# Attention stage: the weighted sum of values right behind each block of scores on TensorE

## The chip, the cores and the metric

The kernel runs on one core of one Trainium2 chip. The metric is the device time of one launch in microseconds, as the median of several runs. The before kernel was run three times.

## What is computed

One layer of a hybrid block on x of 2048 positions by 1024, all in float32. The part that matters here is the attention over a sliding window of two chunks of 64 positions, with 8 query heads and 2 key/value heads:

```python
def window_sink_attention(q, k, v, sinks):
    ...
    qc = q.reshape(B, n_chunks, CHUNK, KV_HEADS, GQA_GROUP, HEAD_DIM)
    kw = chunk_window(k.reshape(B, n_chunks, CHUNK, KV_HEADS, HEAD_DIM))
    vw = chunk_window(v.reshape(B, n_chunks, CHUNK, KV_HEADS, HEAD_DIM))
    scores = jnp.einsum('bnqkgd,bnjkd->bnkgqj', qc, kw).astype(jnp.float32) * scale
    ...
    probs = jax.nn.softmax(jnp.concatenate([scores, sink], axis=-1), axis=-1)[..., :-1]
    out = jnp.einsum('bnkgqj,bnjkd->bnqkgd', probs.astype(v.dtype), vw)
```

Around it stand: z = RMSNorm(x) @ w_in, split into q, k, v and the two halves u and v of a gating unit; rotary embedding of q and k; the gating unit; both parts normalised, concatenated and multiplied by w_out; a residual; and a SwiGLU block of width 2816 with another residual.

## The kernel before, in words

Each engine has its program written out by hand, and semaphores join them. Nothing reorders anything: an instruction starts when those ahead of it on its engine have been issued and its own waits hold. Float32 matrix products are split into a high and a low part, so each product is three matmuls (high x high, high x low, low x high). Pairs of tiles go through a Strassen-like scheme of seven products instead of eight.

The 2048 positions are 16 tiles of 128. The stages on TensorE are: the gating unit's columns of w_in, then the attention stage, in which the product with the q, k, v columns of w_in for pair p = j + 1 is laced with the attention of tiles 2j and 2j + 1, then the product with w_out, then the SwiGLU block's up and down products. The loop of the attention stage (from line 2243) runs over j = 0 to 6, some 22 us each.

The steps for tile k, and the engine of each:

- `rope_products` (VectorE, L1510 and L1517) multiply z by the rope table into `ropeA` and `ropeB`; `rotate` (GpSimd) adds these into `qrot` (L651) and `krot` (L654).
- `turn_qk` (TensorE, L2155 and L2157) transposes `qrot` into PSUM tile `T0` and `krot` into `T1`. It waits for `rot_done`, and for `aO_done`, since `T0` also holds the result of `weighted`.
- `queries` (ScalarE, L933) and `keys` (VectorE, L1526 to L1528) copy these to SBUF.
- `scores` (TensorE, L2172) makes the scores in PSUM tile `S`: 64x64 blocks of the array with 128 columns moving. It waits until both halves of `probsT` of tile k - 1 have been copied.
- `maxima` (VectorE, L1536 to L1543) and `exps` (ScalarE, L942 to L944) make `probs`.
- `turn_probs` (TensorE, L2181) transposes `probs`; one half is copied into `probsT` by ScalarE (L952), the other by VectorE (L1549).
- `weighted` (TensorE, L2196) multiplies `probsT` by the values `vA` and `vB` into `T0`: 128x64 blocks with 64 columns moving, 16 instructions. It waits for `probsT`, for the values, and for `queries` of the tile whose transposes were in `T0`.
- `attended` (VectorE, L1560) divides by the sums of exponentials into `aO` and frees `T0`; then come `squares_A` (ScalarE, L958, L960), `rms_A` (GpSimd, L603) and `mix_A` (VectorE, L1569).

The seven products (`qkv_product(p, i)`, L2141 to L2143) have 12 matmuls each of 128x128 with 384 columns. `qkv_u2` and `qkv_u3` (VectorE, L1476, L1483) read products 2 and 3; `qkv_upper` (VectorE, L1491) reads product 5 and completes z of the next even tile, and `rope_products` of that tile comes right behind it, then `qkv_lower` (L1495), which reads product 6, then `attended(2j)`. Behind `attended(2j)` VectorE has in most iterations one or two operations of another kind: `again_scale` (L1607, at the start of iterations 1 and 3), `wout_lo_part` (L1573, at the start of iterations 2 and 4, and more in 7), `again_sums` (L1615, L1617, iteration 5), `left_lo` (L1261, iteration 6). The prediction names the six moved even blocks by their j, 0 to 5; the operation behind `attended(2j)` then stands at the start of iteration j + 1.

Of the kernel before, what the change touches and what calls it, by code (L numbers as in the profile page):

```python
# [15 lines left out]
TILES = SEQ // P  # L16
# [19 lines left out]
NP = TILES // 2  # L36
# [11 lines left out]
def build_kernel(nc, x, x_q, w_uv, w_qkv, w_out, w_gu, w_dn, gain_in, gain_out, post_mix, pre_ffn,  # L48
# [206 lines left out]
    def chunk(c):  # L255
        return slice(c * P, (c + 1) * P)
# [22 lines left out]
    with block:  # L279
# [1727 lines left out]
        def _(e):  # L2007
# [107 lines left out]
            def qkv_product(p, i, ks=range(HK)):  # L2115
                b, (left, _) = (p + 1) % 2, UP_PRODUCTS[i]
                if ks[0] == 0:
                    if p == 0:
                        e.wait_ge(w_split, 9 + i + 1)
                        if i in (0, 1):  # L2120
                            e.wait_ge(sB_done, 2 * (NP - 1))
                        if i == 2:
                            e.wait_ge(gel_done, 4 * (NP - 1) + 2)
                        if i == 3:
                            e.wait_ge(v12_first, NQ)
                    else:
                        if i == 0 and p < NP - 1:
                            e.wait_ge(hl_in[b], 32 * ((p + 1) // 2))
                        if p == NP - 1 and i in (0, 1, 3):
                            e.wait_ge(lsplit, 3 * NP + (1, 2, 0, 3)[i])  # L2130
                        if i < 4:
                            e.wait_ge((z11_done, v12_first, u2_first, v21_first)[i], (0, NQ, NQ, NQ)[i] + p)
                    if i in (4, 5):
                        e.wait_ge(in_copied, 2 * (NQ + p) + i - 3)
                    if i == 6:
                        e.wait_ge(u3_first, NQ + p + 1)
                bank = QB[BANK[i]]
                for k in ks:
                    w = slice(k * P, (k + 1) * P)
                    hi, lo = lb_hi[b][:, left, w], lb_lo[b][:, left + 1, w]  # L2140
                    e.matmul(bank, hi, wq_hi[i][:, k, :], start=i < 4 and k == 0, stop=False, skip_group_check=True)  # L2141
                    e.matmul(bank, hi, wq_lo[i][:, k, :], start=False, stop=False, skip_group_check=True)
                    ins = e.matmul(bank, lo, wq_hi[i][:, k, :], start=False, stop=k == HK - 1, skip_group_check=True)  # L2143
                if ks[-1] == HK - 1:
                    ins.then_inc(in_done, 1)

            def turn_qk(k):
                e.wait_ge(rot_done, 2 * k + 2)
                if k:
                    e.wait_ge(aO_done, k - 1)  # L2150
                    e.wait_ge(k_done, 3 * k)
                if k == TILES - 2:
                    e.wait_ge(mixT_split, 2)
                for i in range(PAIRS):
                    ins = e.transpose(T0[:, chunk(i)], qrot[:, chunk(i)], ident[:, :])  # L2155
                ins.then_inc(q_full, 1)
                e.transpose(T1[:, 0:P], krot[:, :], ident[:, :]).then_inc(k_full, 1)  # L2157

            def scores(k):
                if k == 0:  # L2160
                    e.wait_ge(pool_consts, 6)
                    e.wait_ge(sB_done, TILES)
                else:
                    e.wait_ge(pTa_done, k)
                    e.wait_ge(pTv_done, k)
                e.wait_ge(qT_done, k + 1)
                e.wait_ge(k_done, 3 * k + 2)
                for i in range(PAIRS):
                    for half, window in enumerate((kA[k % 2], kB)):
                        for kv in range(KVH):  # L2170
                            r = slice(kv * HD, (kv + 1) * HD)
                            ins = e.matmul(S[half * CH:(half + 1) * CH, kv, chunk(i)],  # L2172
                                           qT[r, i * P + half * CH:i * P + (half + 1) * CH], window[r, :],
                                           start=True, stop=True)
                ins.then_inc(s_full, 1)

            def turn_probs(k):
                for i in range(2):
                    e.wait_ge(exp_done, 9 * k + 5 + 4 * i)
                    for c in range(4):  # L2180
                        ins = e.transpose(S[:, i, chunk(c)], probs[:, chunk(4 * i + c)], ident[:, :])  # L2181
                    ins.then_inc(pT_full, 1)

            def weighted(k):
                e.wait_ge(pTa_done, k + 1)
                e.wait_ge(pTv_done, k + 1)
                e.wait_ge(v_done, 3 * k + 3)
                e.wait_ge(qT_done, min(k + 2, TILES))
                if k == TILES - 4:
                    e.wait_ge(mixT_split, 1)  # L2190
                if k == TILES - 2:
                    e.wait_ge(mixT_split, 3)
                for h in range(NH):
                    kv = h // PAIRS
                    for half, vals in enumerate((vA[k % 3], vB[k % 2])):
                        ins = e.matmul(T0[half * CH:(half + 1) * CH, h * HD:(h + 1) * HD],  # L2196
                                       probsT[:, h * P + half * CH:h * P + (half + 1) * CH],
                                       vals[:, kv * HD:(kv + 1) * HD], start=True, stop=True)
                ins.then_inc(pv_done, 1)

            def mix_transposes(k):
                e.wait_ge(mix_in[k % 2], 16 * (k // 2 + 1))
                if k < 2:
                    e.wait_ge(qT_done, TILES - 2 + 2 * k)
                    e.wait_ge(k_done, 3 * (TILES - 2 + 2 * k))
                if k:
                    e.wait_ge(mixT_split, 2 * k)
                if k == 2:
                    e.wait_ge(aO_done, TILES)
                for i in range(2):  # L2210
                    for c in range(4):
                        ins = e.transpose(T[i][:, chunk(c)], mixin[k % 2][:, chunk(4 * i + c)], ident[:, :])
                    ins.then_inc(mixT_full, 1)

            def out_units(k, first, end):
                par = k % 2
                if first == 0:
                    e.wait_ge(mixT_split, 2 * k + 2)
                    if k == 0:
                        e.wait_ge(z11_done, NP)  # L2220
                        e.wait_ge(v12_first, NQ + NP)
                    if k == 1:
                        e.wait_ge(u2_first, NQ + NP)
                        e.wait_ge(v21_first, NQ + NP)
                    if k >= 2:
                        e.wait_ge(y_done, k - 1)
                for unit in range(first, end):
                    c, a = unit // 2, unit % 2
                    w = slice(a * 512, (a + 1) * 512)
                    if k == 0 and a == 0:  # L2230
                        e.wait_ge(wout_split, c + 1)
                    ins = three(M[par][:, a, :], mixT_hi[par][:, chunk(c)], mixT_lo[par][:, chunk(c)],
                                wout_hi[c][:, w], wout_lo[c][:, w], c == 0, c == KD - 1)
                    if k == TILES - 1 and c in (3, 4) and a == 1:
                        ins.then_inc(wout_half, 1)
                if end == 2 * KD:
                    ins.then_inc(mm2_full, 1)
# [5 lines left out]
            for j in range(NP - 1):  # L2243
                p = j + 1
                qkv_product(p, 0)
                turn_qk(2 * j)
                if j:
                    turn_probs(2 * j - 1)
                qkv_product(p, 1, range(0, 2))
                scores(2 * j)  # L2250
                qkv_product(p, 1, range(2, 4))
                qkv_product(p, 2)
                if j:
                    weighted(2 * j - 1)
                qkv_product(p, 3)
                turn_qk(2 * j + 1)
                qkv_product(p, 4, range(0, 2))
                turn_probs(2 * j)
                qkv_product(p, 4, range(2, 4))
                scores(2 * j + 1)  # L2260
                if p == NP - 1:
                    mix_transposes(0)
                qkv_product(p, 5)
                qkv_product(p, 6)
                weighted(2 * j)
            out_units(0, 0, 2)
            turn_probs(TILES - 3)
            out_units(0, 2, 5)
# [151 lines left out]
```

## Time and profile before

| what | value |
|---|---|
| runs | 1850.42, 1850.9, 1851.03 us |
| median | 1850.9 us |
| profiled execution, first to last instruction (its span) | 1849.8 us |
| TensorE busy | 1824.4 us, 99% of the span |
| VectorE busy | 1273.8 us, 69% |
| ScalarE busy | 743.1 us, 40% |
| GpSimd busy | 154.0 us, 8% |
| attention stage | about 203 to 402 us |

The profile is of one execution on the one core. A time of its own outside the span is not listed for it, so the span stands for it. Busy means that at least one instruction is in the engine; for TensorE the granted clock is at full speed in all 40 slices. A matmul's listed duration is its latency; the pace at which matmuls follow each other is read from their starts. Behind most rows of a timeline nothing stands; "[0.24 <-PE T L2196]" says that the engine was idle for 0.24 us ahead of it and that the matmuls of line 2196 on tile T ended that.

### The profile page before, as it was taken

What the parts mean: (1) busy time and instruction counts of PE and PEld (TensorE: products, weight loads), DVE (VectorE), ACT (ScalarE), POOL (GpSimd) and SP (SyncE); (2) the same over time, 40 slices, a digit from 0 to 9 for tenths busy, and PEclk for the clock granted to TensorE, in tenths of its full rate; (3) what the DMA queues carried; (4) which work ended last, traced back from release to release, by engine and by line L of the source; (5) the groups of instructions that cost most, each with busy time, mean ns of one, the idle gap of its engine ahead of it and who ended that gap; (6) DMA issues with size and microseconds to landing.
All of it is one profiled execution on the core that took longest, in us unless ns stands there. A gap on an engine that the chain in (4) does not pass through costs nothing.

```text
span 1849.8 us, 24806 instructions
## 1 busy us (share of the span) xinstructions
PE 1824.4 (99%) x9322; PEld 1526.0 (82%) x9322; DVE 1273.8 (69%) x1625; ACT 743.1 (40%) x1279; POOL 154.0 (8%) x162
## 2 busy tenths in 40 slices
PE   9999899999999999999999999999999999999998
PEld 7788899978888888888888888888887888888887
DVE  7878877864458867676777767777677756554574
ACT  7776566753345332323224332322323222232342
POOL 1211222211000000000000000000000000000244
PEclk9999999999999999999999999999999999999999
DMA  6787645245576323332235423333234754535655
GB/s 229 291 291 276 238 186 198 92 160 193 200 274 246 139 85 108 122 101 95 85 110 196 148 85 99 114 105 108 85 108 166 268 219 163 189 132 179 244 203 190
DMA packets 134324, 310.78 MB, mean 168 GB/s; under 512 B 6384, under 2 KB 85232, under 8 KB 121072
## 3 DMA queue, kind: packets, MB, share of 16 engines
q1 hardware_dynamic: 134256, 309.90, 47.8%
q8 instruction: 40, 0.66, 0.1%
q14 instruction: 28, 0.23, 0.0%
HBM read 207.64 MB, written 102.24 MB: 168 GB/s over the span
## 4 chain that ended last, share of the span: by engine, by line
PE 75%; DVE 2%; issue 0%; POOL 0%; ACT 0%; DVEq 0%; POOLq 0%
PE T L2010 7%; PE T L2012 7%; PE T L2011 7%; PE ZB L2332 4%; PE ZB L2334 4%; PE ZB L2333 4%; PE T L2334 4%; PE T L2332 4%; PE T L2333 4%; PE S L2334 3%; PE S L2332 3%; PE S L2333 3%; PE ZA L2334 3%; PE ZA L2332 3%; PE ZA L2333 3%; PE ZA L2012 1%
## 5 line engine op out<-in xcount | busy, mean ns | idle before, releaser
L2010 PE MATMUL T<-tb_hi,sb_hi 128*128 128x512 f32 x616 | 239.9, 390 | 1.5 <-DVE sb_lo L1896 1.2
L2012 PE MATMUL T<-tb_hi,sb_lo 128*128 128x512 f32 x616 | 239.7, 389 | 0.0
L2011 PE MATMUL T<-tb_lo,sb_hi 128*128 128x512 f32 x616 | 239.6, 389 | 0.0
L1184 ACT ACTIVATE sb_hi<-sb_raw 128x1408 fp32r<-128x1408 f32 x56 | 77.4, 1382 | 291.0 <-PE T L2012 275.6
L1759 DVE TENSOR_TENSOR t_lo<-t_raw,t_hi 128x1024 fp32r<-128x1024 f32 (+1 forms) x126 | 168.9, 1396 | 0.1
L2010 PEld LDWEIGHTS T<-tb_hi,sb_hi 128*128 128x128 f32 x616 | 115.6, 188 | 26.6 <-issue 2.1
L2332 PE MATMUL ZB<-s_hi,t_hi 128*128 128x512 f32 x352 | 137.1, 389 | 0.3 <-DVE t_lo L1759 0.3
L2332 PE MATMUL T<-s_hi,t_hi 128*128 128x512 f32 x352 | 137.0, 389 | 0.0
L2334 PE MATMUL T<-s_hi,t_lo 128*128 128x512 f32 x352 | 136.9, 389 | 0.0
L2334 PE MATMUL ZB<-s_hi,t_lo 128*128 128x512 f32 x352 | 136.9, 389 | 0.0
L2333 PE MATMUL ZB<-s_lo,t_hi 128*128 128x512 f32 x352 | 136.9, 389 | 0.0
L2333 PE MATMUL T<-s_lo,t_hi 128*128 128x512 f32 x352 | 136.9, 389 | 0.0
L2011 PEld LDWEIGHTS T<-tb_lo,sb_hi 128*128 128x128 f32 x616 | 115.7, 188 | 24.0
L2012 PEld LDWEIGHTS T<-tb_hi,sb_lo 128*128 128x128 f32 x616 | 115.6, 188 | 23.9
L1896 DVE TENSOR_TENSOR sb_lo<-sb_raw,sb_hi 128x1408 fp32r<-128x1408 f32 x56 | 96.2, 1717 | 34.5 <-ACT sb_hi L1184 34.5
L1124 ACT ACTIVATE th<-v 128x512 f32<-128x512 f32 x66 | 41.8, 633 | 192.2 <-DVE v L1785 90.1
L702 POOL TENSOR_TENSOR rstdf<-msf,mhalf 128x1 f32<-128x1 f32 x16 | 14.5, 904 | 1182.2 <-ACT msf L1193 1180.0
L1111 ACT ACTIVATE p<-T 128x512 f32<-128x512 f32 x22 | 13.2, 598 | 245.5 <-PE T L2334 245.5
L2332 PE MATMUL ZA<-s_hi,t_hi 128*128 128x512 f32 x264 | 102.7, 389 | 0.0
L2333 PE MATMUL ZA<-s_lo,t_hi 128*128 128x512 f32 x264 | 102.7, 389 | 0.0
L2332 PE MATMUL S<-s_hi,t_hi 128*128 128x512 f32 x264 | 102.7, 389 | 0.0
L2333 PE MATMUL S<-s_lo,t_hi 128*128 128x512 f32 x264 | 102.7, 389 | 0.0
(311 smaller groups left out, 4283.6 us busy)
## 6 DMA issues: line engine op xcount, KB each, us to landing
t_raw<-w_gu SPq DMA_DIRECT2D x42, 1024.0 KB, 4.7
act_d<-ac SPq DMA_DIRECT2D x22, 1792.0 KB, 8.0
sb_raw<-act_d SPq DMA_DIRECT2D x56, 704.0 KB, 4.1
h_d<-quarters SPq DMA_DIRECT2D x8, 1792.0 KB, 6.6
s_raw<-h_d SPq DMA_DIRECT2D x14, 1024.0 KB, 6.3
lb_hi<-hl_d SPq DMA_DIRECT2D x6, 1792.0 KB, 7.2
lb_lo<-hl_d SPq DMA_DIRECT2D x6, 1792.0 KB, 10.7
tb_raw<-w_dn SPq DMA_DIRECT2D x6, 1536.0 KB, 6.5
```

The source lines that it names most:

```text
L702: e.tensor_tensor(rstdf[:, f % 2:f % 2 + 1], msf[:, f % 2:f % 2 + 1], mhalf[:, 0:1], ALU.pow).then_inc(rstdf_ready, 1)
L1111: e.activation(p1[:, :], GU[u][0], ACT.Copy).then_inc(pcopy_done, 1)
L1124: e.activation(th[i][:, :], src, ACT.Tanh, scale=0.5).then_inc(th_done, 1)
L1184: e.activation(sb_hi[it % 2][:, :, :], sb_raw[it % 2][:, :, :], ACT.Copy).then_inc(sb_hi_done, 1)
L1759: e.tensor_tensor(t_lo[u][:, first:end, :], t_raw[u][:, first:end, :], t_hi[u][:, first - 1:end - 1, :].bitcast(F32), ALU.subtract).then_i ...
L1896: e.tensor_tensor(sb_lo[it % 2][:, :, :], sb_raw[it % 2][:, :, :], sb_hi[it % 2][:, :, :].bitcast(F32), ALU.subtract).then_inc(sb_split, 1)
L2010: e.matmul(out_ap, lhi, rhi, start=start, stop=False)
L2011: e.matmul(out_ap, lhi, rlo, start=False, stop=False)
L2012: return e.matmul(out_ap, llo, rhi, start=False, stop=stop)
L2332: e.matmul(bank, hi, s_hi[i][:, :, w], start=i < 4 and k == 0, stop=False, skip_group_check=True)
L2333: e.matmul(bank, hi, s_lo[i][:, :, w], start=False, stop=False, skip_group_check=True)
L2334: ins = e.matmul(bank, lo, s_hi[i][:, :, w], start=False, stop=k == HK - 1, skip_group_check=True)
```

## The change

On TensorE alone, in the attention stage's loop, `weighted` goes to another place. `weighted(2j - 1)` stood behind product 2 of the next pair and now stands right behind `scores(2j)`. `weighted(2j)` stood behind product 6, at the end of the iteration, and now stands right behind `scores(2j + 1)`, ahead of products 5 and 6. The last iteration (p = 7) keeps `weighted(12)` behind product 6; there `mix_transposes(0)` stays behind `scores(13)`. So six blocks of odd tiles (1, 3, 5, 7, 9, 11) and six of even tiles (0, 2, 4, 6, 8, 10) move. No instruction is added or taken away, and waits stay as they were.

```diff
                 qkv_product(p, 1, range(0, 2))
                 scores(2 * j)
+                if j:
+                    weighted(2 * j - 1)
                 qkv_product(p, 1, range(2, 4))
                 qkv_product(p, 2)
-                if j:
-                    weighted(2 * j - 1)
                 qkv_product(p, 3)
                 turn_qk(2 * j + 1)
                 qkv_product(p, 4, range(0, 2))
                 turn_probs(2 * j)
                 qkv_product(p, 4, range(2, 4))
                 scores(2 * j + 1)
-                if p == NP - 1:
+                if p < NP - 1:
+                    weighted(2 * j)
+                else:
                     mix_transposes(0)
                 qkv_product(p, 5)
                 qkv_product(p, 6)
-                weighted(2 * j)
+            weighted(TILES - 4)
```

TensorE before, from `scores(3)` to `turn_qk(4)` (S and T0 are the PSUM tiles, wq_hi5, wq_hi6 and wq_hi0 the weights of products 5, 6 and 0; of each run of like rows the first and last stand):

```order
L2172 MATMUL S<-kB_150,qT_147 64x128 x2
L2141 MATMUL ZA<-wq_hi5_122,lb_hi1_75 128x384
...
L2141 MATMUL ZB<-wq_hi6_123,lb_hi1_75 128x384
...
L2196 MATMUL T0<-vA2_153,probsT_157 64x64
...
L2141 MATMUL ZA<-wq_hi0_117,lb_hi0_74 128x384
...
L2155 MATMUL T0<-ident_253,qrot_146 128x128 x4
```

The `weighted` block stands between product 6 and product 0. Now:

```order
L2172 MATMUL S<-kB_150,qT_147 64x128 x2
L2196 MATMUL T0<-vA2_153,probsT_157 64x64
...
L2141 MATMUL ZA<-wq_hi5_122,lb_hi1_75 128x384
...
L2141 MATMUL ZB<-wq_hi6_123,lb_hi1_75 128x384
...
L2141 MATMUL ZA<-wq_hi0_117,lb_hi0_74 128x384
...
L2155 MATMUL T0<-ident_253,qrot_146 128x128 x4
```

The block has moved ahead of product 5, and between product 5 and the turn only products 6 and 0 are left. For the odd tiles, TensorE before, from `scores(2)` to product 3:

```order
L2172 MATMUL S<-kB_150,qT_147 64x128 x2
L2141 MATMUL ZA<-wq_hi1_118,lb_hi1_75 128x384
...
L2141 MATMUL ZB<-wq_hi2_119,lb_hi1_75 128x384
...
L2196 MATMUL T0<-vA1_152,probsT_157 64x64
...
L2141 MATMUL ZB<-wq_hi3_120,lb_hi1_75 128x384
```

And now:

```order
L2172 MATMUL S<-kB_150,qT_147 64x128 x2
L2196 MATMUL T0<-vA1_152,probsT_157 64x64
...
L2141 MATMUL ZA<-wq_hi1_118,lb_hi1_75 128x384
...
L2141 MATMUL ZB<-wq_hi2_119,lb_hi1_75 128x384
...
L2141 MATMUL ZB<-wq_hi3_120,lb_hi1_75 128x384
```

Here the block has moved ahead of the second half of product 1 and of product 2. The order of the other engines' instructions is the same as before.

## Rows read from the trace of the kernel before

**Rows 1.** The page, busy us, share of the span, instructions of each engine.
```profile
PE 1824.4 (99%) x9322; PEld 1526.0 (82%) x9322; DVE 1273.8 (69%) x1625; ACT 743.1 (40%) x1279; POOL 154.0 (8%) x162
```

**Rows 2.** Line 2155 (`turn_qk`): what ended its engine's idle time, us, times.
```profile
  POOL krot L654: 3.1, 5
```

**Rows 3.** Timeline, `weighted(3)`: start us, duration us, engine, line, operation, out<-in.
```profile
239.56 0.33 PE L2142 MATMUL ZB<-wq_lo,lb_hi 128*128 128x384 f32 x1
239.73 0.34 PE L2143 MATMUL ZB<-wq_hi,lb_lo 128*128 128x384 f32 x1
240.00 0.27 PE L2196 MATMUL T<-vA,probsT 128*64 128x64 f32 x1
...
240.93 0.22 PE L2196 MATMUL T<-vB,probsT 128*64 128x64 f32 x1
...
241.08 0.44 PE L2141 MATMUL ZB<-wq_hi,lb_hi 128*128 128x384 f32 x1
241.36 0.34 PE L2142 MATMUL ZB<-wq_lo,lb_hi 128*128 128x384 f32 x1
```

**Rows 4.** Timeline of TensorE, the end of `scores(5)` and the next product.
```profile
270.50 0.28 PE L2172 MATMUL S<-kB,qT 64*64 64x128 f32 x2
270.71 0.44 PE L2141 MATMUL ZA<-wq_hi,lb_hi 128*128 128x384 f32 x1
```

**Rows 5.** Timeline of TensorE at the stage's end, `scores(15)` and `weighted(14)`.
```profile
389.12 0.28 PE L2172 MATMUL S<-kB,qT 64*64 64x128 f32 x2
389.32 0.27 PE L2196 MATMUL T<-vA,probsT 128*64 128x64 f32 x1
```

**Rows 6.** Timeline at j = 5, VectorE's copy of `probsT` and the start of `scores(11)`.
```profile
336.95 0.68 DVE L1549 COPY probsT<-S 128x512 f32<-128x512 f32 x1
...
337.76 0.33 PE L2172 MATMUL S<-kA,qT 64*64 64x128 f32 x2
```

**Rows 7.** Timeline at j = 2, from product 5 to `turn_qk(6)`.
```profile
273.10 0.56 DVE L1491 TENSOR_TENSOR z<-ZA,au 128x384 f32<-128x384 f32 x1 [0.47 <-PE ZA L2143]
...
275.65 1.28 POOL L651 TENSOR_TENSOR qrot<-ropeA,ropeB 128x512 f32<-128x512 f32 x1 [4.91 <-DVE ropeB L1517]
...
276.28 0.69 DVE L1560 TENSOR_TENSOR aO<-T,rden 128x512 f32<-128x512 f32 x1 [0.24 <-PE T L2196]
...
276.88 1.22 DVE L1607 TENSOR_TENSOR xa_raw<-xa_raw,gq 128x1024 f32<-128x1024 f32 x1
276.89 1.53 POOL L654 TENSOR_TENSOR krot<-ropeA,ropeB 128x128 f32<-128x128 f32 x1
...
278.18 0.34 PE L2143 MATMUL ZA<-wq_hi,lb_lo 128*128 128x384 f32 x1
...
278.47 0.33 PE L2155 MATMUL T<-ident,qrot 128*128 128x128 f32 x1
```

**Rows 8.** Timeline at j = 1, from product 5 to `turn_qk(4)`.
```profile
250.47 0.56 DVE L1491 TENSOR_TENSOR z<-ZA,au 128x384 f32<-128x384 f32 x1 [0.49 <-PE ZA L2143]
...
254.26 1.55 DVE L1573 SCALAR_TENSOR_TENSOR wout_lo<-wout_raw,gcol_out,wout_hi 128x1024 fp32r<-128x1024 f32 x1
254.27 0.46 POOL L654 TENSOR_TENSOR krot<-ropeA,ropeB 128x128 f32<-128x128 f32 x1
...
255.72 0.60 PE L2155 MATMUL T<-ident,qrot 128*128 128x128 f32 x4
```

**Rows 9.** Timeline at j = 6, GpSimd's rotation and VectorE's `wout_lo`.
```profile
368.35 1.29 POOL L651 TENSOR_TENSOR qrot<-ropeA,ropeB 128x512 f32<-128x512 f32 x1 [6.69 <-DVE ropeB L1517]
368.65 2.07 DVE L1573 SCALAR_TENSOR_TENSOR wout_lo<-wout_raw,gcol_out,wout_hi 128x1024 fp32r<-128x1024 f32 x1
369.59 1.45 POOL L654 TENSOR_TENSOR krot<-ropeA,ropeB 128x128 f32<-128x128 f32 x1
```

**Rows 10.** Timeline at j = 4, the same two engines.
```profile
322.34 0.68 DVE L1615 TENSOR_TENSOR lb_raw<-xa_raw,xa_raw 128x512 f32<-128x512 f32 x1
322.34 1.00 POOL L654 TENSOR_TENSOR krot<-ropeA,ropeB 128x128 f32<-128x128 f32 x1
```

## Prediction

> **What bounds the kernel now.** I read the page's busy shares first: TensorE is busy for 1824.4 of 1849.8 us, so its own sequence of instructions, plus the few places where it waits, is the time [rows 1]. The page's row of granted clock is at full speed in every slice, so no term here hangs on the clock. The edit reaches only the loop of the attention stage, about 205 to 370 us, where tile k's `turn_qk`, `turn_probs`, `scores` and `weighted` are laced between the seven products of the next pair. Second I read who made the transposes of `turn_qk` wait: five times GpSimd's `krot`, 3.1 us in all with the weight loads' waits [rows 2]; three of them are turns of this loop. The profile thus names GpSimd's rotation as the wait that already ends last at some turns. Third come the timelines at one joint of each kind, to price what is moved; last, those of VectorE and GpSimd in front of a waiting turn.
>
> **What a `weighted` block costs where it stands now.** The last product matmul starts at 239.73, the block's first at 240.00, its last at 240.93; the next product starts at 241.08, its second matmul at 241.36 [rows 3]. That is 0.27 + 0.93 + 0.15 + 0.28 = 1.63 us. Without the block the same two steps are two product pitches of 0.17 (239.56 to 239.73), 0.35 us. The block costs 1.28 us: 0.93 of its own and 0.35 of entering and leaving. All twelve moved blocks read alike.
>
> **What it costs behind `scores`.** From the last `scores` to a product is 0.21 us, with the slow second step behind it too [rows 4]. At the end of the stage the kernel already has a `scores` with a `weighted` right behind, and there that step is 0.20 us [rows 5]. In its new place a block adds 0.20 + 0.93 + 0.15 - 0.21 = 1.07 us; the slow second step is paid once, where it was paid twice. A joint therefore saves 1.28 - 1.07 = 0.21 us of TensorE's own time, and twelve save 2.5 us. That much the change gives by itself.
>
> The Trainium skill, "TensorEngine Tiling (Array Packing)", Key Properties, says that changing the tiling mode drains TensorE. Products, `scores` (64x64) and `weighted` (128x64) are three shapes, so by this rule the joint keeps three of four drains; the trace agrees in kind, since 0.20 us stays between the two small blocks.
>
> **The odd tiles: the saving stays.** `weighted(2j-1)`, six blocks, moves inside the stretch from `scores(2j)` to `scores(2j+1)`. Its data are there, because `scores(2j)` waits for the same halves of `probsT`. Its reader on VectorE, `attended`, has `qkv_u2` ahead of it, which waits for product 2 and now comes 1.07 us later; `attended` ends some 1.5 us behind product 2's last matmul, and the next `turn_qk`, which waits for it, is 2.4 us behind. So 0.8 us of cover is left. `scores(2j+1)` waits a little for `probsT`, but that chain starts at `turn_qk(2j+1)`, which moves with TensorE. One exception, at j = 5: VectorE has extra sums behind `attended`, so `qkv_u3` loses the start 0.21 us earlier, and from there VectorE runs without a gap up to the copy of `probsT` that starts at 336.95; `scores(11)` starts at 337.76, right behind it [rows 6]. I take 0.2 us off. Sum: 6 x -0.21 + 0.2 = -1.05 us.
>
> **The even tiles: the cover of GpSimd's rotation goes.** `weighted(2j)`, six blocks (j = 0 to 5), stood behind product 6, between product 5 and `turn_qk(2j+2)`. It now stands ahead of product 5. But product 5 starts a chain that ends in that turn: VectorE adds `z` (L1491, 273.10), multiplies by the rope table, GpSimd adds `qrot` from 275.65 to 276.93 and `krot` from 276.89 to 278.42, and `turn_qk` starts at 278.47 [rows 7]. I count from the start U of L1491. The chain lets the turn start at U + 5.37 here, while TensorE would have been ready 0.12 us sooner, at U + 5.25 (a turn that does not wait follows the product by 0.17, this one by 0.29). The change takes 1.28 us out of TensorE's side of this race and nothing out of the chain's: TensorE is ready at U + 3.97, and the turn still comes when `krot` is done. The 1.07 us ahead of product 5 moves U itself later and is paid in full.
>
> What does the chain take then? `krot` lasts 1.53 us here and not its median 0.46, since VectorE's operation with two SBUF inputs started 0.01 us ahead of it, and it ended 0.32 us behind that operation's end at 278.10 [rows 7]. At j = 1 (and 3) the order is the other way: `wout_lo` and `krot` start within 0.01 us, `krot` lasts 0.46 and ends at U + 4.26, a whole 1 us before the turn at U + 5.25 [rows 8]. After the change this cannot stay: `attended` waited 0.24 us for the `weighted` block [rows 7] and now need not, so the VectorE operation behind it starts at least that much sooner, while `qrot` still runs. The one place of that kind is j = 6: `wout_lo` came 0.30 us after `qrot`'s start, took 2.07 us, and `krot` ended at 371.04, which is 1.40 us behind `qrot`'s end at 369.64 [rows 9]. With that row as price, `krot` ends at U + 3.83 + 1.40 and the turn starts at U + 5.28, for j = 0, 1, 2, 3 and 5. For j = 4 the VectorE operation takes 0.68 and not 1.27 us [rows 10], so U + 4.69.
>
> Against the distances of now this is -0.09 for j = 0, 2, 5 (5.37 before), +0.03 for j = 1, 3 and -0.56 for j = 4 (5.25 before). A turn that waited is also 0.05 us longer than one that did not (the block of five transposes reads 0.49 against 0.44 between first and last start), new for j = 1, 3, 4: +0.15. Sum of the even tiles: 6 x 1.07 - 0.27 + 0.06 - 0.56 + 0.15 = +5.8 us. TensorE then waits some 1.3 us at five turns and 0.7 at one. Nothing behind takes this back: what follows a turn (`keys`, `queries`, copies of `probsT`) hangs on it, the loads of the next pair are issued a whole pair ahead, and the later stages are TensorE's.
>
> Bounds. If `krot` kept its place ahead of `wout_lo` at j = 1 and 3, each of these turns would start at U + 4.31, 2 x 0.97 = 1.9 us less. If it went first everywhere, the even tiles would cost 6 x 1.07 + 3 x (4.31 - 5.37) + 3 x (4.31 - 5.25) + 0.15 = +0.6. If VectorE's operation had to wait out `qrot` and then took its whole 1.22 to 1.27 us, where row 9 shows 1.08 left of it, 0.15 to 0.2 us is added at five turns, +0.9. I take row 9, the only one in which VectorE's operation comes while `qrot` runs.
>
> The Trainium skill, "SBUF — State Buffer", Who interferes with whom, states that a VectorE instruction with two SBUF inputs and a GpSimd one that reads SBUF block each other for the whole instruction, by order of issue. By this rule it would be the upper bound of the paragraph above; row 9's 2.07 us is less than a whole wait (0.99) and a whole operation (1.27), so the row stands.
>
> **Total.** +5.8 - 1.05 = +4.8 us on the profiled span of 1849.8, so a span near 1854.6. The median of three runs, 1850.9, lies 1.1 us over the span, which I carry over: 1855.7 us, 0.26% slower. A measurement of this kernel can tell about 0.2%, 3.7 us, from no change.
>
> **Rivals.**
> - *`krot` stays first at j = 1 and 3.* It ended 1 us before its turn now, and 0.01 us decides who goes first. For it: [rows 8] itself. Against: VectorE's operation starts at least 0.24 us sooner. Time: 4.8 - 1.9 = +2.9 us, 1853.8.
> - *No joint waits, only the saving shows (not slower).* It decides at 1.3 us: the chain from product 5 to `krot` would have to end by U + 3.97. For it: TensorE's own time does fall by 12 x 0.21. Against: even with no VectorE operation in its way the chain ends at U + 4.26. Time: -2.5 us, 1848.4; with the freed `krot` everywhere +0.6 - 1.05, about 1850.5.
> - *The joints save nothing and the block is total.* The 0.20 us of [rows 5] is one place, ahead of other products. If the new joints cost what two entries cost, the odd tiles give 0 instead of -1.05, the even ones 1.28 instead of 1.07, and +0.9 comes from the full block: 4.8 + 1.05 + 1.3 + 0.9 = +8.0, 1858.9.
> - *The change does not do what it says.* The order shows TensorE's rows moved as told and no other engine's, so only its worth is open.
>
> **How the numbers follow.** The forecast (1855.7, from +3.8 to +6.2) gets 0.6, `krot` first 0.2, the two forms without a cost together 0.11, the dear joint 0.06, something that gains more than 3.7 us 0.03. The range runs from 1852.7 to 1857.8: it holds the forecast and the first rival with the full block's bound, about 0.84. Slower by over 0.2% needs more than 3.7 us: 0.6 + 0.06, 0.66. Within 0.2%: 0.31. Faster: 0.03.
>
> **What would show it.** Right: `turn_qk` waits for `krot` at six even turns, 0.7 to 1.4 us each, where three waited 0.12; `krot` lasts over 1 us at j = 1 and 3; `scores` to `weighted` reads 0.20 and the second step behind the pair 0.28; the stretch from `turn_qk(2j)` to `turn_qk(2j+2)` is longer by 0.3 to 1.0 us. Wrong: `krot` at 0.46 with a small wait (first rival), or a turn 0.17 us behind product 0 (second). A new wait of a product, of `scores` or of VectorE's `keys` on something else would mean that I missed a chain.

## The result and the profile after

The changed kernel takes 1856.35 us (median of 7 runs, 1855.85 to 1857.37) against 1851.03 us (7 runs) of the kernel before: ratio 1.0028, 95% interval 1.0019 to 1.0037, so about 5.3 us slower. The profiled span is 1854.6 us against 1849.8, +4.8.

The page of the changed kernel, busy us of each engine, beside [rows 1]:

```profile
PE 1823.9 (98%) x9322; PEld 1527.5 (82%) x9322; DVE 1274.0 (69%) x1625; ACT 743.7 (40%) x1279; POOL 154.9 (8%) x162
```

TensorE is busy for 0.5 us less and the span is 4.8 us longer: what was added is waiting. The waits of TensorE between 225 and 365 us in the changed kernel (engine, tile, line, whom it waited for: us in all, times, longest), where the kernel before lists none:

```profile
PE T L2155 <- POOL krot L654: 6.5, 6, 1.2
PE S L2172 <- ACT probsT L952: 0.2, 1, 0.2
```

Six turns of even tiles wait for GpSimd's `krot`. The timeline of the changed kernel at j = 1, to be laid beside [rows 8] (start us, duration us, engine, line, operation, in brackets the idle time before it and its releaser):

```profile
252.96 0.56 DVE L1491 TENSOR_TENSOR z<-ZA,au 128x384 f32<-128x384 f32 x1 [1.57 <-PE ZA L2143]
...
255.51 1.29 POOL L651 TENSOR_TENSOR qrot<-ropeA,ropeB 128x512 f32<-128x512 f32 x1 [6.01 <-DVE ropeB L1517]
...
255.81 0.68 DVE L1560 TENSOR_TENSOR aO<-T,rden 128x512 f32<-128x512 f32 x1
256.41 1.47 DVE L1573 SCALAR_TENSOR_TENSOR wout_lo<-wout_raw,gcol_out,wout_hi 128x1024 fp32r<-128x1024 f32 x1
...
256.75 0.34 PE L2143 MATMUL ZA<-wq_hi,lb_lo 128*128 128x384 f32 x1
256.76 1.44 POOL L654 TENSOR_TENSOR krot<-ropeA,ropeB 128x128 f32<-128x128 f32 x1
...
258.25 0.66 PE L2155 MATMUL T<-ident,qrot 128*128 128x128 f32 x4 [1.16 <-POOL krot L654]
```

`attended` (L1560) no longer has an idle time ahead of it, so `wout_lo` starts at 256.41, while `qrot` runs until 256.80 (255.51 + 1.29). `krot`, which lasted 0.46 us in [rows 8], now lasts 1.44, and the turn starts 5.29 us behind L1491; it was 5.25. TensorE's last product matmul had started at 256.75, 1.50 us before the turn, where 0.17 is no wait. At j = 4 the operation in front is the short one, beside [rows 10]:

```profile
327.29 0.93 DVE L1615 TENSOR_TENSOR lb_raw<-xa_raw,xa_raw 128x512 f32<-128x512 f32 x1
...
327.63 0.91 POOL L654 TENSOR_TENSOR krot<-ropeA,ropeB 128x128 f32<-128x128 f32 x1
```

And the new joint, `scores(3)` with `weighted(2)`, beside [rows 4, 5]:

```profile
249.26 0.28 PE L2172 MATMUL S<-kB,qT 64*64 64x128 f32 x2
249.47 0.27 PE L2196 MATMUL T<-vA,probsT 128*64 128x64 f32 x1
...
250.40 0.22 PE L2196 MATMUL T<-vB,probsT 128*64 128x64 f32 x1
250.55 0.45 PE L2141 MATMUL ZA<-wq_hi,lb_hi 128*128 128x384 f32 x1
250.83 0.34 PE L2142 MATMUL ZA<-wq_lo,lb_hi 128*128 128x384 f32 x1
```

0.21 + 0.93 + 0.15 us, and the slow second step of 0.28 once: the joint is as cheap as foreseen.

### The profile page after: what moved, and what is told of

Read it like the earlier page. It is cut to its first block, busy times and chain, and to the rows that moved or that the text cites. A ratio compares the mean times of both kernels' runs of the same rounds, so it can differ in the third digit from the quotient of the medians.

```text
span 1854.6 us, 24806 instructions
## 1 busy us (share of the span) xinstructions
PE 1823.9 (98%) x9322; PEld 1527.5 (82%) x9322; DVE 1274.0 (69%) x1625; ACT 743.7 (40%) x1279; POOL 154.9 (8%) x162
## 4 chain that ended last, share of the span: by engine, by line
PE 76%; DVE 3%; ACT 1%; issue 0%; POOL 0%; DVEq 0%; POOLq 0%; ACTq 0%
PE T L2010 7%; PE T L2012 7%; PE T L2011 7%; PE ZB L2334 4%; PE ZB L2336 4%; PE ZB L2335 4%; PE T L2336 4%; PE T L2334 4%; PE T L2335 4%; PE S L2336 3%; PE S L2334 3%; PE S L2335 3%; PE ZA L2336 3%; PE ZA L2334 3%; PE ZA L2335 3%; PE ZB L2010 2%
## 5 line engine op out<-in xcount | busy, mean ns | idle before, releaser
L2336 PE MATMUL ZA<-s_hi,t_lo 128*128 128x512 f32 x264 | 102.7, 389 | 0.0
```

What stands on the lines that cost most here:

```text
L2336: ins = e.matmul(bank, lo, s_hi[i][:, :, w], start=False, stop=k == HK - 1, skip_group_check=True)
```

## The experiments

Nine kernels ran, eleven times each (e2 six times), beside runs of the kernel before on the same chip. A median here can tell about 1.7 us from no change (2.4 in e2), so small differences are also read from the profile, as the time from the start of `turn_qk(0)` to the start of `turn_probs(15)`, the attention stage without what lies around it. That stretch is 182.83 us before (212.49 to 395.32) and 187.81 in the changed kernel (213.08 to 400.89).

| kernel | median, us | against before | ratio, 95% interval | stretch, us | against before |
|---|---|---|---|---|---|
| the change | 1856.35 | +5.3 | 1.0019 to 1.0037 | 187.81 | +4.98 |
| e1_odd_only | 1849.69 | -1.1 | 0.9987 to 1.0005 | 181.80 | -1.03 |
| e2_even_only | 1856.75 | +5.95 | 1.0020 to 1.0045 | 188.82 | +5.99 |
| e3_after_krot_first | 1850.37 | -0.4 | 0.9990 to 1.0008 | 182.39 | -0.44 |
| e4_after_ops_later | 1851.95 | +1.15 | 0.9997 to 1.0015 | 183.81 | +0.98 |
| e5_even_behind_product5 | 1850.17 | -0.3 | 0.9989 to 1.0007 | 182.23 | -0.60 |
| e6_odd_krot_first | 1849.10 | -1.4 | 0.9983 to 1.0001 | 181.34 | -1.49 |
| e7_after_probs_first | 1849.15 | -1.35 | 0.9983 to 1.0001 | 181.17 | -1.66 |
| e8_all_parts | 1848.31 | -2.2 | 0.9979 to 0.9997 | 180.60 | -2.23 |
| e9_krot_first | 1849.88 | -0.7 | 0.9988 to 1.0006 | 182.07 | -0.76 |

(Before, on the three chips: 1850.8 for e1 to e4, 1850.5 for e5 to e7, 1850.54 for e8 and e9.)

**The two halves of the change, each alone: e1 and e2.**

The edit of e1, to the kernel before:

```diff
                 scores(2 * j)
+                if j:
+                    weighted(2 * j - 1)
                 qkv_product(p, 1, range(2, 4))
                 qkv_product(p, 2)
-                if j:
-                    weighted(2 * j - 1)
```

And that of e2, to the kernel before:

```diff
                 scores(2 * j + 1)
-                if p == NP - 1:
+                if p < NP - 1:
+                    weighted(2 * j)
+                else:
                     mix_transposes(0)
                 qkv_product(p, 5)
                 qkv_product(p, 6)
-                weighted(2 * j)
+            weighted(TILES - 4)
```

> The kernel before with only the six odd blocks, weighted(2j-1), moved behind scores(2j). Theory (the joint saves TensorE 0.21 us each, and the loss is all on the even side): about -1.0 us against before, the stretch from scores(2j) to scores(2j+1) shorter by 0.2 us, and the waits on krot as before (three of 0.12 us). Rival (a block behind scores costs more than it saves, in both places): +2 us or more.

> The kernel before with only the six even blocks, weighted(2j), moved behind scores(2j+1), ahead of product 5. Theory (the block goes to the other side of product 5, whose chain through VectorE and GpSimd sets the even turn): +5.8 us against before, all in waits of turn_qk(2j+2) on krot, 1.2 us at five turns and 0.6 at one. Rival (the joint itself is dear): the stretch lengthens in TensorE's own steps, and odd and even blocks each bring half of the loss.

Measured: -1.1 and +5.95 us; in the stretch -1.03 and +5.99, together +4.96, for +4.98 of the whole change. In e1 the way from `scores(2j)` to `scores(2j+1)` is 11.19 us (235.88 to 247.07) from `scores(2)` and 11.21 to 11.29 from the others, where it was 11.38 or 11.39. In e2 the waits between 225 and 365 us are these alone:

```profile
PE T L2155 <- POOL krot L654: 6.4, 6, 1.2
```

The loss is all on the even side, and there it is the turn's wait.

**Is it the end of GpSimd's rotation? e3 and e4.** e3 swaps the two additions of `rotate` in the changed kernel; e4 takes VectorE's operation away from them.

```diff
+                e.tensor_tensor(krot[:, :], ropeA[:, AW:AW + P], ropeB[:, AW:AW + P], ...)
                 e.tensor_tensor(qrot[:, :]..., ALU.add).then_inc(rot_done, 1)
-                e.tensor_tensor(krot[:, :], ropeA[:, AW:AW + P], ropeB[:, AW:AW + P], ...)
```

> The changed kernel with GpSimd's two additions in the other order, krot (0.46 us) ahead of qrot (1.28 us); the turn still waits for both. Theory (the chain ends at krot because VectorE's next operation with two SBUF inputs gets in ahead of it): qrot is already running when that operation comes, so both additions end by U + 4.27 (U is the start of VectorE's L1491), the turn starts at U + 4.32 in all six iterations and waits 0.35 us, -5.3 us against the changed kernel, -0.5 against before. Rival (the chain is long whatever the order, and contention only shifts it): the turn stays at U + 5.29 and nothing is gained.

```diff
                     attended(2 * j - 2)
-                if j in (1, 3):
-                    again_scale(j // 2)
-                if j in (2, 4):
-                    wout_lo_part(j // 2 - 1)
...
                         attended(2 * j - 1)
+                    if j in (1, 3):
+                        again_scale(j // 2)
+                    if j in (2, 4):
+                        wout_lo_part(j // 2 - 1)
```

> The changed kernel with VectorE's extra operations of iterations 1 to 4 (again_scale and wout_lo_part, 1.2 to 1.3 us each) moved from behind attended(2j-2) to behind attended(2j-1), away from the rotation. Theory (these operations hold up krot): krot lasts 0.46 us at these four turns, they start at U + 4.31, 0.98 us sooner each, -3.9 us against the changed kernel, +1 against before; the turns of the last two stay at U + 4.75 and U + 5.29. Rival (krot is slow for another reason): krot stays at 1.44 us and the time does not move.

Measured: e3 is 0.4 us under the kernel before, e4 1.15 us over it. The turns start 4.30 to 4.32 us behind L1491 in all six iterations of e3, and 4.30 or 4.31, then 4.76 and 5.30, in e4. The timeline of e3 at j = 1:

```profile
253.68 0.46 POOL L651 TENSOR_TENSOR krot<-ropeA,ropeB 128x128 f32<-128x128 f32 x1 [5.98 <-DVE ropeB L1517]
254.09 1.28 POOL L653 TENSOR_TENSOR qrot<-ropeA,ropeB 128x512 f32<-128x512 f32 x1
254.58 1.88 DVE L1573 SCALAR_TENSOR_TENSOR wout_lo<-wout_raw,gcol_out,wout_hi 128x1024 fp32r<-128x1024 f32 x1
...
255.43 0.44 PE L2155 MATMUL T<-ident,qrot 128*128 128x128 f32 x2 [0.18 <-POOL qrot L653]
```

`wout_lo` still comes while `qrot` runs, and now it alone pays (1.88 us; in e5, where it meets no GpSimd addition, it lasts 1.27), off the path. Swapping two lines takes back all of the loss. e3 is also the case that the prediction priced as "with the freed `krot` everywhere", +0.6 - 1.05: the stretch reads -0.44.

**Is it the side of product 5? e5.**

```diff
                 qkv_product(p, 5)
-                qkv_product(p, 6)
+                if p == NP - 1:
+                    qkv_product(p, 6)
                 weighted(2 * j)
+                if p < NP - 1:
+                    qkv_product(p, 6)
```

> The kernel before with the six even blocks moved past product 6 only, between products 5 and 6, so they stay on the same side of product 5. Theory: TensorE has the same work between product 5 and the even turn, so the time is that of before within 0.5 us; attended(2j) no longer waits, VectorE's next operation therefore starts while qrot runs, and krot rises from 0.46 to 1.44 us at j = 1 and 3 at no cost, since the turn comes at U + 5.25 anyway. Rival (any move of these blocks towards scores costs): +2 us or more.

The time is that of before, as foreseen, and the turn starts 5.24 or 5.25 us behind L1491 in all six iterations. The part on `krot` was a miss: it lasts 0.46 or 0.47 us everywhere, at j = 0, 2, 4 and 5 too, which also removes the three small waits. I had forgotten that `qkv_lower` (L1495) reads product 6, which now ends a block later:

```profile
253.65 0.56 DVE L1495 TENSOR_TENSOR z<-ZB,au 128x384 f32<-128x384 f32 x1 [0.89 <-PE ZB L2143]
254.08 0.46 POOL L654 TENSOR_TENSOR krot<-ropeA,ropeB 128x128 f32<-128x128 f32 x1
254.12 0.68 DVE L1560 TENSOR_TENSOR aO<-T,rden 128x512 f32<-128x512 f32 x1
254.72 1.27 DVE L1573 SCALAR_TENSOR_TENSOR wout_lo<-wout_raw,gcol_out,wout_hi 128x1024 fp32r<-128x1024 f32 x1
```

VectorE waits 0.89 us for product 6, so `wout_lo` comes behind `krot`. `attended`, whose first input lies in PSUM, holds no addition up: in e3 `qrot` starts at 254.09, inside `attended` (253.98 to 254.66), and still lasts 1.28 us.

**A better kernel: e6, e9, e7 and e8.** e6 is e1 with the swap of e3, e9 the kernel before with the swap alone.

> The kernel before with the odd blocks moved and krot ahead of qrot; the even blocks stay. Theory: the odd joints give 1.0 us, and the three waits of 0.12 us at even turns go too, so -1.4 us against before. Rival (order on GpSimd matters nothing where the turn is not waiting): -1.0.

> The kernel before with krot ahead of qrot and nothing else. Theory (the rotation's end is late only at the three even turns that wait 0.12 us): these waits go, -0.4 us against before, and e6 minus e1 is the same 0.4. Rival (the order on GpSimd has an effect of its own elsewhere, as on the turns of odd tiles): more than 1 us either way.

Measured -1.4 and -0.7 us (stretch -1.49 and -0.76). Three waits of 0.12 and three turns 0.05 us shorter make 0.5, but neither kernel shows just that. In e9 the six steps from `scores(2j + 1)` to `scores(2j + 2)`, j = 0 to 5, are 0.60 us shorter in all, and the one from `scores(14)` to `scores(15)` 0.12 us: the 0.4 foreseen was too small. e6 is 0.46 us of stretch under e1 because two things offset each other: it gains these 0.12 us too and loses 0.16 where `scores(12)` to `scores(13)` takes 11.40 us for 11.24, and the profile lists a wait of 0.2 us of a product's weight load for VectorE's `lb_lo` (L1261). All these are differences far below what a median can tell.

e7 keeps all twelve blocks in their new places and puts `turn_probs(2j-1)` in front of the even turn as its cover. Besides this edit it has the swap of e3, and the copies of `probsT` stand ahead of `queries` and `keys`.

```diff
                 qkv_product(p, 0)
-                turn_qk(2 * j)
                 if j:
                     turn_probs(2 * j - 1)
+                turn_qk(2 * j)
```

> The changed kernel with krot ahead of qrot and, at the even turns, turn_probs(2j-1) ahead of turn_qk(2j) on TensorE, with the copies of probsT ahead of those of the turn on ScalarE and VectorE. Theory: 0.8 us of transposes stand in front of the turn, so TensorE reaches it at U + 4.76 and GpSimd's end at U + 4.27 is hidden; all twelve joints then show their 0.21 us, -2.5 us against before and -7.5 against the changed kernel. Rival: the wait moves on to scores(2j), which now has only half a product between it and the turn whose copies it needs, 0.2 to 0.5 us each, and half of the gain or all of it is lost.

It gives -1.35 us instead of -2.5. For e7 and e8, j is the iteration, whose even turn is that of tile 2j. The waits on GpSimd are gone from the loop, but `scores(2j)` comes 0.43 us behind its product (0.64 at j = 5), so a part of the rival holds. VectorE and `scores(6)` at j = 3 of that kernel:

```profile
277.02 1.89 DVE L1605 TENSOR_TENSOR xa_raw<-xa_raw,gq 128x1024 f32<-128x1024 f32 x1
278.83 0.68 DVE L1547 COPY probsT<-S 128x512 f32<-128x512 f32 x1
...
279.74 0.25 DVE L1524 COPY kB<-T 128x128 f32<-128x128 f32 x1
279.83 0.34 PE L2141 MATMUL ZA<-wq_hi,lb_lo 128*128 128x384 f32 x1
...
280.26 0.33 PE L2170 MATMUL S<-kA,qT 64*64 64x128 f32 x2
```

`again_scale`, drawn out to 1.89 us behind `qrot`, pushes the copy of `probsT` and that of the keys. e8 also moves these operations, as e4 does.

> The kernel of e7_after_probs_first with VectorE's extra operations of iterations 1 to 4 also moved behind attended(2j-1), as in e4_after_ops_later. In the kernel of e7, scores(2j) came 0.43 to 0.64 us behind the product ahead of it at the even tiles of j = 1 to 5, where 0.27 is no wait. Theory (these waits are for copies that the extra operation on VectorE pushes back): at j = 1 to 4 the gap returns to 0.27, -0.7 us against e7, about -2.0 against before, and the gap of 0.64 at j = 5 stays. Rival (the copies are late because they follow the turn, whatever stands ahead on VectorE): the gaps stay at 0.43 and the time is that of e7, -1.35 against before.

```profile
277.92 0.69 DVE L1547 COPY probsT<-S 128x512 f32<-128x512 f32 x1 [1.51 <-PE S L2179]
...
278.83 0.25 DVE L1524 COPY kB<-T 128x128 f32<-128x128 f32 x1
...
279.14 0.34 PE L2141 MATMUL ZA<-wq_hi,lb_lo 128*128 128x384 f32 x1
...
279.41 0.33 PE L2170 MATMUL S<-kA,qT 64*64 64x128 f32 x2
```

The copy of `probsT` now waits for TensorE and not for an operation of VectorE, and that of the keys comes early enough behind it; the gaps at j = 1 to 4 are 0.27 us, that of j = 5 stays at 0.61. e8 takes 1848.31 us, 2.2 us under the kernel before, and its interval excludes 1; its stretch is 7.2 us under that of the changed kernel. Not all of this is the joints': the swap alone gives 0.76 us of stretch (e9), and e8 is 1.47 us under e9, where twelve joints of 0.21 were to give 2.5. Against e9 eight of the twelve save 0.17 to 0.19 us each. The other four show less or none: the steps up to `scores(10)`, `scores(11)`, `scores(12)` and `scores(13)` change by +0.15, -0.12, -0.02 and -0.06 us, and the first three of these still start 0.61, 0.49 and 0.33 us behind the matmul ahead (e9: 0.27, 0.41, 0.27).

## Why the prediction was right

- *TensorE's own price.* A block costs 1.28 us alone and 1.07 behind `scores`: the new joints read 0.20 or 0.21 us at all twelve places, and with odd blocks alone moved (e1) the saving of some 0.2 us per tile is the whole effect. In the changed kernel the five plain odd stretches are 0.17 or 0.18 us shorter each, foreseen 0.21.
- *The exception at j = 5* was mis-sized. `scores(11)` comes 0.49 us behind its product instead of 0.41, and its stretch is still 0.10 us shorter (11.29 for 11.39), where I had written off the whole 0.2. The odd sum is -1.03 us for -1.05 foreseen: the two small errors cancel.
- *The even turns.* The turns start at U + 5.28 or 5.29 at j = 0, 1, 2, 3 and 5 and at U + 4.75 at j = 4; foreseen were 5.28 and 4.69. That [rows 9] was the right row for VectorE's operation coming while `qrot` runs is what decided between +2.9 and +4.8: `krot` lasts 1.44 us at j = 1 and 3. e3 and e4 show the mechanism: where VectorE's operation no longer comes between the additions (six turns of e3, four of e4), the turn starts at U + 4.30 to 4.32. The even sum is +5.99 us (e2) for +5.8.
- *The waits.* From the product's last start to the turn it is 1.50 us at five turns and 0.97 at one, 1.33 and 0.80 over the 0.17 of no wait; foreseen some 1.3 and 0.7. The profile lists 1.16 and 0.63 of it, since it counts from the product's end.
- *Total.* The span is 1854.6 us, as forecast. That it fits to the digit is in part luck, since the stretch grew by 4.98, and outside it the two executions differ by 0.2 us the other way. The forecast of +4.8 lies inside the measured interval of 3.5 to 6.9 us. The 0.65 us by which 1856.35 is over the forecast come from the step from span to time: in the seven runs of the changed kernel the time is 1.75 to 1.85 us over the span, where the prediction carried over 1.1, the difference between the median of three runs and the span of one execution.

What stays open: why at j = 1, in the kernel before, GpSimd was served first where both engines' operations started within 0.01 us [rows 8], and VectorE at j = 2 [rows 7]. e1 repeats all six outcomes. In both kernels `krot` goes first against `wout_lo` (scalar_tensor_tensor, 4 of 4) and second against the tensor_tensor operations L1607, L1615 and L1261 (8 of 8). So the outcome goes with the kind of operation, but each kind also has iterations of its own, and no run put the same kind at both places: the cause is not shown. Nor did I follow the last 0.61 us gap at j = 5 of e8 beyond the profile, which names VectorE's copy of the keys.

## What to carry to other kernels

Before moving work on the busiest engine, ask on which side of the producer of each running chain it stands: 1.28 us of matmuls behind product 5 was free cover for a chain of VectorE and GpSimd, and the same work ahead of product 5 delayed that chain. A joint that saves 0.2 us is worth having only where the cover can be spared; e8 got most of it by putting other work (the transposes of the probabilities) in the place. And where a late step waits for two results of one engine, do the short one first: swapping two lines on GpSimd gave back the whole 5 us. It helped only where the other engine's operation came once the long one was running. Before the turn of tile 14 in e3 `wout_lo` starts at 368.13, ahead of `qrot` (368.25), which then lasts 2.31 us, and the rotation ends at U + 5.27, no sooner than in the changed kernel (U + 5.23); the turn there comes at U + 6.51, so this cost nothing.

## What the runs showed of the hardware

- A VectorE operation of 1.21 to 1.27 us with two SBUF inputs that comes while GpSimd adds two SBUF tiles ends 1.07 to 1.09 us behind GpSimd's end wherever it came 0.3 to 0.9 us after the start of `qrot`; for `wout_lo` (1.27 us undisturbed, in e5) 370.72 - 369.64 [rows 9], 257.88 - 256.80 in the changed kernel, 256.46 - 255.37 in e3. It is held, but some 0.2 us of it are over by then. `again_scale` and `left_lo` (1.21 to 1.22 us where nothing holds them) end as far behind, so only 0.12 to 0.14 us of these are over, and L1615 (0.68 us) ends 0.54 or 0.55 behind. The Trainium skill, "SBUF — State Buffer", Who interferes with whom, has the later one fully blocked until the other ends; the trace agrees but for these 0.1 to 0.2 us.
- A GpSimd addition that comes meanwhile ends 0.32 us behind VectorE's end, 258.20 against 257.88, where it lasts 0.46 us undisturbed.
- Where both start within 0.01 us, either can go first: `krot` won at j = 1 and 3 and lost at j = 0, 2, 4 and 5 of the kernel before.
